# Loads of small tables moved behind a stage's first weight units, x issued from ScalarE's queue

## What is computed

```python
for l in range(2):                                          # first_block
    h = h + 0.5 * swiglu(rms_norm(h, ffn1_norm[l]), ...)    # f1
    h = h + token_mixer(rms_norm(h, mix_norm[l]), ...)      # m
    h = h + 0.5 * swiglu(rms_norm(h, ffn2_norm[l]), ...)    # f2
x = rms_norm(h, final_norm)
for l in range(2):                                          # second_block
    x = x + 0.5 * rmsnorm(swiglu_2(rmsnorm(x, ffn1_pre_g[l]), ...), ffn1_post_g[l])
    ...                                                     # mixer, with mix_post_g
    x = x + 0.5 * rmsnorm(swiglu_2(rmsnorm(x, ffn2_pre_g[l]), ...), ffn2_post_g[l])
```

## Time and profile before

| | |
|---|---|
| median of three runs | 2842.36 us |
| the profiled execution | 2840.82 us, its span 2839.0 us |
| PE busy | 2639.4 us (93%) |
| DVE, ACT busy | 1544.9 us (54%), 1223.6 us (43%) |
| mean granted TensorE clock | 0.958 |
| HBM read | 452.84 MB, 161 GB/s over the span |

### The profile page before, as it was taken

One profiled execution on the slowest core, in us unless ns is written; L12 is line 12 of the kernel. 1 busy time (PEld: TensorE's weight loads), 2 busy tenths in 40 slices (PEclk: granted clock), 3 DMA queues, 4 the chain that ended last, 5 costly groups with the idle time before them and its releaser, 6 DMA issues.

```text
span 2839.0 us, 30036 instructions
## 1 busy us (share of the span) xinstructions
PE 2639.4 (93%) x12238; PEld 2196.0 (77%) x12238; DVE 1544.9 (54%) x1787; ACT 1223.6 (43%) x1530; POOL 48.2 (2%) x71
## 2 busy tenths in 40 slices
PE   7799999989998998898998998899898998998899
PEld 5688778878887887786877877688687877877687
DVE  3445665455565554555556575555454556475544
ACT  3445444444453443444434453444444444453443
POOL 0000000000000000000000000000000000000000
PEclk9899999999999999999998999999999998999999
DMA  7665355555643555655542442554664552432553
GB/s 183 195 226 174 112 167 186 178 169 187 215 163 119 178 190 165 199 185 170 180 169 90 135 134 75 171 192 140 196 192 170 178 164 96 135 134 75 170 183 129
DMA packets 309753, 459.02 MB, mean 162 GB/s; under 512 B 18112, under 2 KB 207856, under 8 KB 309360
## 3 DMA queue, kind: packets, MB, share of 16 engines
q1 hardware_dynamic: 307552, 453.95, 48.8%
q10 hardware_dynamic: 2064, 3.15, 1.0%
HBM read 452.84 MB, written 4.19 MB: 161 GB/s over the span
## 4 chain that ended last, share of the span: by engine, by line
PE 85%; DVE 5%; ACT 3%; DMA 3%; issue 2%; SPq 1%; DVEq 0%; POOL 0%; ACTq 0%
PE acc L586 45%; PE work L586 32%; PE work L593 2%; PE acc L797 2%; ACT w_hi L1024 2%; DMA raw<-ffn_w_dram 1%; PE work L781 1%; DMA raw<-w_ffn_in_dram 1%; DVE w_lo L1331 1%; PE work L993 1%; DVE xt_lo L1355 1%; SPq L366 0%; DVE field L1519 0%; DMA raw<-w_in_dram 0%; PE work L810 0%
## 5 line engine op out<-in xcount | busy, mean ns | idle before, releaser
L1331 DVE TENSOR_TENSOR w_lo<-raw,w_hi 128x2048 fp32r<-128x2048 f32 (+1 forms) x420 | 953.5, 2272 | 879.8 <-ACT w_hi L1024 879.4
L1024 ACT CAST w_hi<-raw 128x2048 fp32r<-128x2048 f32 (+1 forms) x420 | 794.6, 1893 | 693.8 <-PE acc L586 294.6
L586 PE MATMUL work<-w_hi,xt_hi 128*128 128x512 f32 x1408 | 563.7, 400 | 66.8 <-DVE xt_lo L1355 63.8
L586 PE MATMUL work<-w_hi,xt_lo 128*128 128x512 f32 x1408 | 553.8, 393 | 0.0
L586 PE MATMUL work<-w_lo,xt_hi 128*128 128x512 f32 x1408 | 553.4, 393 | 0.0
L586 PE MATMUL acc<-w_hi,yt_hi 128*128 128x512 f32 x1088 | 435.6, 400 | 21.6 <-DVE yt_lo L1342 20.9
L586 PE MATMUL acc<-w_lo,yt_hi 128*128 128x512 f32 x1088 | 430.4, 396 | 0.0
L586 PE MATMUL acc<-w_hi,yt_lo 128*128 128x512 f32 x1088 | 430.0, 395 | 0.0
L586 PE MATMUL acc<-w_hi,xt_hi 128*128 128x512 f32 (+2 forms) x896 | 347.7, 388 | 24.4 <-DVE xt_lo L1355 20.0
L586 PEld LDWEIGHTS work<-w_hi,xt_hi 128*128 128x128 f32 x1408 | 268.0, 190 | 125.5 <-issue 72.6
L586 PE MATMUL acc<-w_hi,xt_lo 128*128 128x512 f32 (+2 forms) x896 | 343.9, 384 | 0.0
(11 more groups left out here) (162 smaller groups left out, 1708.3 us busy)
## 6 DMA issues: line engine op xcount, KB each, us to landing
raw<-ffn_w_dram SPq DMA_DIRECT2D x264, 512.0 KB, 4.5
raw<-w_in_dram SPq DMA_DIRECT2D x204, 512.0 KB, 4.5
raw<-w_ffn_in_dram SPq DMA_DIRECT2D x176, 512.0 KB, 4.8
raw<-w_ffn_out_dram SPq DMA_DIRECT2D x88, 512.0 KB, 4.4
raw<-w_branch_dram SPq DMA_DIRECT2D x48, 512.0 KB, 4.5
raw<-w_out_dram SPq DMA_DIRECT2D x32, 512.0 KB, 4.4
bias<-b_gate_dram SPq DMA_DIRECT2D x10, 512.0 KB, 7.6
raw<-w_branch_attn_dram SPq DMA_DIRECT2D x8, 512.0 KB, 4.0
```

The source lines that it names most:

```text
L586: last = nc.tensor.matmul(out, x[:, kt, k], y, start=start and n == 0, stop=stop and n == 2)
L1024: nc.scalar.copy(w_hi[:, slot, 0:n], raw[:, at, 0:n]).then_inc(hi_split[slot], 1)
L1331: nc.vector.tensor_tensor(w_lo[:, at, 0:n], raw[:, at, 0:n], w_hi[:, slot, 0:n].bitcast(F32), ALU.subtract).then_inc(unit_split[slot], 1)
```

## The change

The small loads of a stage are issued behind its fifth unit (u+4) rather than its second; in `mixer2` behind its fourth. The tables that stood between the blocks are issued with those of the first stage of block 1. The constants and `final_norm` are issued behind the fifth unit of stage 0; x, `ident` and the first gain come from ScalarE's queue, and ACT and DVE turn the first half of row 0 before they split unit 0. The bias table is made at step j = 2 rather than j = 0, in another PSUM bank, and PE no longer waits for its reader.

```diff
             def ffn(block, name, l, between=lambda: None):
                 load(u, gate_up(block, name, l, 0, 0))
                 load(u + 1, gate_up(block, name, l, 0, 4))
-                small(block, l, name)
                 for j in range(steps - 1):
                     load(u + 3 * j + 2, gate_up(block, name, l, j + 1, 0))
                     load(u + 3 * j + 3, gate_up(block, name, l, j + 1, 4))
                     load(u + 3 * j + 4, down(block, name, l, j))
+                    if j == 0:
+                        small(block, l, name)
+                        between()
...
-                chunks("w_in_2", 2576, 1)
+                chunks("w_in_2", 2576, 2)
                 small(1, l, "m")
-                chunks("w_in_2", 3088, 3)
+                chunks("w_in_2", 3600, 2)
...
-            for r in range(2):
-                sp.dma_start(h[:, r, :], a["x"][0, r * P:(r + 1) * P, :]).then_inc(x_loaded[r], 16)
-            sp.dma_start(ident[:, :], a["ident"]).then_inc(ident_loaded, 16)
-            sp.dma_start(vec[:, 0:8], a["gain1"][0]).then_inc(gain1_loaded, 16)
...
+            def constants():
+
+                sp.dma_start(field[0:32, 4096:4112], a["rel_bias_2"]).then_inc(consts_loaded, 16)
...
+                sp.dma_start(post[:, :], a["final_norm"].rearrange("(a n) -> a n", a=1).partition_broadcast(P)) \
+                    .then_inc(post_loaded, 16)
+
+            def second_block():
+
+                sp.wait_ge(h_ready, h_count(number[0, depth - 1, "f2"]))
+                for dst, src in ((decay, a["decay"]), (rope2, a["rope2"])):
+                    sp.dma_start(dst, src).then_inc(blk_loaded, 16)
+                sp.wait_ge(scratch_stored, 16)
...
             for block in range(2):
                 for l in range(depth):
-                    ffn(block, "f1", l)
+                    ffn(block, "f1", l, (second_block if block else constants) if l == 0 else lambda: None)
...
                     if j == 0:
                         turn_hidden(0)
-                        if stage == 0:
-                            pe.wait_ge(consts_loaded, 80)
-                            nc.tensor.matmul(acc[0][0:16, 0:3 * P], field[0:32, 4096:4112], field[0:32, 4200:4584],
+                    if j == 2 and stage == 0:
+                        pe.wait_ge(consts_loaded, 80)
+                        nc.tensor.matmul(work[1][0:16, 0:3 * P], field[0:32, 4096:4112], field[0:32, 4200:4584],
...
-                    if j == 0 and stage == 0:
-                        pe.wait_ge(table_ready, 2)
...
+                elif not stage:
+                    split(0)
                 turn_hi_rows(stage, 0, (2, 3))
+                if not stage:
+                    split(1)
                 split(u + 2)
...
-            split(0)
-            split(1)
+            act.dma_start(h[:, 0, :], a["x"][0, 0:P, :]).then_inc(x_loaded[0], 16)
+            act.dma_start(ident[:, :], a["ident"]).then_inc(ident_loaded, 16)
+            act.dma_start(vec[:, 0:8], a["gain1"][0]).then_inc(gain1_loaded, 16)
+            act.dma_start(h[:, 1, :], a["x"][0, P:2 * P, :]).then_inc(x_loaded[1], 16)
             enter(0)
...
-                    elif stage == 0:
+                    if j == 2 and stage == 0:
                         act.wait_ge(table_ready, 2)
                         act.dma_start(a["scratch"], field[0:16, 5000:5384].unsqueeze(1).broadcast_to([16, P, 3 * P])) \
                             .then_inc(scratch_stored, 16)
```

More of the change, by code:

```diff
@@ L419, in mixer_small, with ffn @@
                         .then_inc(bias_loaded[i], 16)
-            def ffn(block, name, l):
+            def ffn(block, name, l, between=lambda: None):
                 u = first_unit[block, l, name]
@@ L498, in mixer2 @@
                 chunks("w_out_2", 0, 2)
-            for r in range(2):
-                sp.dma_start(h[:, r, :], a["x"][0, r * P:(r + 1) * P, :]).then_inc(x_loaded[r], 16)
-            sp.dma_start(ident[:, :], a["ident"]).then_inc(ident_loaded, 16)
-            sp.dma_start(vec[:, 0:8], a["gain1"][0]).then_inc(gain1_loaded, 16)
-            sp.dma_start(field[0:32, 4096:4112], a["rel_bias_2"]).then_inc(consts_loaded, 16)
-            sp.dma_start(field[0:32, 4200:4584], a["one_hot"]).then_inc(consts_loaded, 16)
@@ L506, in _ @@
-            sp.dma_start(field[0:16, 4600:4984], a["unseen"]).then_inc(consts_loaded, 16)
-            sp.dma_start(causal[:, :], a["causal"]).then_inc(consts_loaded, 16)
-            sp.dma_start(rope1[:, :, :, :], a["rope1"]).then_inc(consts_loaded, 16)
+            def constants():
+                sp.dma_start(field[0:32, 4096:4112], a["rel_bias_2"]).then_inc(consts_loaded, 16)
+                sp.dma_start(field[0:32, 4200:4584], a["one_hot"]).then_inc(consts_loaded, 16)
+                sp.dma_start(field[0:16, 4600:4984], a["unseen"]).then_inc(consts_loaded, 16)
+                sp.dma_start(causal[:, :], a["causal"]).then_inc(consts_loaded, 16)
+                sp.dma_start(rope1[:, :, :, :], a["rope1"]).then_inc(consts_loaded, 16)
+                sp.dma_start(post[:, :], a["final_norm"].rearrange("(a n) -> a n", a=1).partition_broadcast(P)) \
+                    .then_inc(post_loaded, 16)
@@ new lines, in second_block @@
+            def second_block():
[3 more added lines that the diff above has]
+                sp.wait_ge(scratch_stored, 16)
+                sp.dma_start(rel_bias, bass.AP(a["scratch"].tensor, P - 1,
+                                               [[3 * P - 1, P], [3 * P * P, 16], [1, 2 * P]])) \
+                    .then_inc(blk_loaded, 16)
@@ L509, in _ @@
             for block in range(2):
                 for l in range(depth):
-                    ffn(block, "f1", l)
+                    ffn(block, "f1", l, (second_block if block else constants) if l == 0 else lambda: None)
                     (mixer2 if block else mixer1)(l)
                     ffn(block, "f2", l)
[L514 to L523, removed]
-                                                   [[3 * P - 1, P], [3 * P * P, 16], [1, 2 * P]])) \
-                        .then_inc(blk_loaded, 16)
@@ L698, in ffn @@
                         turn_hidden(0)
-                        if stage == 0:
-                            pe.wait_ge(consts_loaded, 80)
-                            nc.tensor.matmul(acc[0][0:16, 0:3 * P], field[0:32, 4096:4112], field[0:32, 4200:4584],
-                                             start=True, stop=True).then_inc(table_ready, 1)
+                    if j == 2 and stage == 0:
+                        pe.wait_ge(consts_loaded, 80)
+                        nc.tensor.matmul(work[1][0:16, 0:3 * P], field[0:32, 4096:4112], field[0:32, 4200:4584],
+                                         start=True, stop=True).then_inc(table_ready, 1)
                     for r in range(2):
                         gate_up_rows(u + 2 + 3 * j, j, 1, r)
-                    if j == 0 and stage == 0:
-                        pe.wait_ge(table_ready, 2)
                     for r in range(2):
@@ L1438, in enter @@
                 else:
-                    turn_lo_rows(stage, 0, range(4))
+                    turn_lo_rows(stage, 0, (0, 1))
+                    split(0)
+                    turn_lo_rows(stage, 0, (2, 3))
+                    split(1)
                 split(u + 2)
@@ L1476, in ffn @@
                         split(u + 5 + 3 * j)
-                    elif stage == 0:
+                    if j == 2 and stage == 0:
                         dve.wait_ge(table_ready, 1)
-                        nc.vector.tensor_tensor(field[0:16, 5000:5384], acc[0][0:16, 0:3 * P], field[0:16, 4600:4984],
+                        nc.vector.tensor_tensor(field[0:16, 5000:5384], work[1][0:16, 0:3 * P], field[0:16, 4600:4984],
                                                 ALU.add).then_inc(table_ready, 1)
```

## The result

The kernel after takes **2754.59 us**, the median of four runs (2753.86 to 2757.64), beside 2841.57 for the kernel before in the same comparison (four runs): a ratio of 0.9698, with an interval of 0.9676 to 0.972. That is 87.0 us less. The forecast was 2754.0. The profiled execution of after took 2757.64 us, span 2755.9, at a mean granted clock of 0.970. The two profiled executions lie 83.1 us apart in their spans.

A forecast was written before the change was run, and what follows sets the result against it. PE was taken to bound the kernel wherever fed, leaving only its idles to win. Boundaries 75.4, switch 6.9, stage 6's tables -0.4, start 6.0 and store 0 sum to 87.9 us less: 2754 us, range 2736 to 2779.

The forecast's parts named there:

- The bound: Whole kernel: PE bounds it wherever fed (85% of the ending chain), so the change wins only where PE stands still.
- Boundaries: Starts of stages 3 and 6 to 11: a unit not yet multiplied holds up `xt_lo`; freeing it gains 75.4 us.
- the forecast's walk: Stage 11, all four engines followed from h at 2638.67: `turn_hidden` at 2654.0 against 2664.38, 10.4 us gained.
- a sign of being wrong: Anywhere: u+5 or the load from scratch becomes the end of PE's waits, or the store's gap moves over 8 us.
- The switch: Between the blocks: PE's 4.2 us wait and 2.7 us of slow products both go, 6.9 us gained.
- The start: Program start: first product at about 12.9 us, 6.0 us earlier, bounds 4.2 to 7.5.
- the rival of 4.2 us by issue time alone: Program start: the second queue saves only issue time, 4.2 us, total 2755.8; chance 0.12.
- The store: Bias table's store in stage 0, costing 20.1 us: moving it from j = 0 to j = 2 gains 0, between -15 and +8.
- The rival of a changed price: Bias table's store: up to 15 us less (2739) or 5.6 us more (2760); chance 0.12.
- The slower rival: Whole kernel: a denser PE is granted less clock, say 0.90 instead of 0.958, giving 2904 us; chance 0.01.
- The boundary rival: Stage starts: boundaries give less, as u+5 lands late or the silu chain is longer; 2778 us, chance 0.18.
- The signs named in advance: Trace: `xt_lo` waits about 1 us, no stage-start cast awaiting DMA, first product near 13 us, 36 us store near 70.

The follow-up runs named there:

- e4: Kernel after with one tiny ScalarE activation ahead of its first real one, to bring the table load forward; 2751.69 us.
- e8: Kernel after with row 0 of x, `ident` and first gain on SyncE's queue ahead of weights, row 1 of x behind unit 1; 2751.37 us.
- e7: Kernel after with store in four parts, block 1's tables spread over stage 6, x on SyncE's queue, and a tiny activation at the start; 2729.25 us.

## Why the prediction was right, and where it was not

**The bound.** Right. PE bound the kernel wherever it was fed, and the edit of the small loads, which touches no product, gave 79.9 us by itself through the seven starts of stages.

**Boundaries.** Right in mechanism and size: 75.0 forecast, 75.7 in the traces. PE resumes 0.77 us late in stage 11 (0.9 forecast), and the clock level of 0.50 behind it is gone, as forecast. In stage 11 the chain from h to `turn_hidden` takes 2581.22 - 2566.87 = 14.35 us, the forecast's walk had 2654.0 - 2638.67 = 15.3, so the silu chain is one us shorter than walked and the boundary gives 11.6, not 10.4. In stage 6 the cover was less than forecast: u+5 lands at 1118.46 + 9.66 = 1128.12, 17.7 us behind h rather than 14.6, and PE waits 2.75 us for it rather than at most 1. The boundary gives 9.85 where 11.9 was counted. What failed in the walk is the start of the tables and not the rate: it counted them as begun when h is complete (1110.4) at 0.35 MB per us, but the windows of after (columns of rows 6) show 153 GB/s in the first five us and 363 in the next, the rate of the earlier trace rows and more.

```profile
1110.00:1115.00 5.00, 4.24 (x22) 3.12 (x22) 4.70 (x10) 5.00 (x13) 3.50 (x4) 1.00 0.54 153
1115.00:1120.00 5.00, 5.00 (x24) 4.14 (x23) 4.36 (x3) 3.15 (x4) 0.00 (x0) 1.00 1.03 363
```

By an estimate from these windows, the 1.0 MB that the first five us moved less than at 0.35 MB per us are 2.8 of the 3.1 us by which u+5 was late. The prediction had named this as a sign of being wrong, "if u+5 or the load from scratch became the end of PE's waits": in stage 6, and only there, u+5 did.

**The switch.** The term of 6.9 us was too large: 3.9. PE now stands for h itself, and behind that the clock is not full: its transposes wait 1.86 us for the final norm's `h`, and the granted clock from 1100 to 1105 us is 0.66 (PE's timeline, the window, columns of rows 6).

```profile
1100.57 1.14 PE L623 MATMUL work<-ident,h 128*128 128x128 f32 x6 [1.86 <-DVE h L1413]
```
```profile
1100.00:1105.00 5.00, 4.42 (x16) 3.51 (x17) 3.16 (x8) 1.14 (x4) 0.00 (x0) 0.66 0.41 139
```

The forecast added the idle and the slow products and did not ask what is late next, though it did so at every boundary. It also put both down to the tables as one; about 2 us of the idle were `final_norm`'s.

**The start.** The term of 6.0 us failed: the pair of traces gives 3.8, just under its lower bound of 4.2, and the means of three and seven executions 40.0 - 35.9 = 4.1. That is near the rival of 4.2 us by issue time alone, but the agreement says nothing for that rival: unit 0, whose first issue moved up by 4.2 us, was cast only 2.1 us earlier in `e4` (8.99, against 11.05), and the order of ACT's and DVE's work changed as well. The walk had `xt_hi` ready before unit 0 was cast. It took all DMAs of the start as one sum of bytes at a common rate, by which the small `ident` would be there early, and it took ACT's table load as hidden, because it was so in before. Both were on the path. Repairing either brought `turn_hidden(0)` to 33.8 and 33.4 us, against 35.9 on the mean.

**The store.** The 0 for its move was right, and so was its price as a whole (20.1 read from the trace, 18 to 20 shown by splitting it). The rival of a changed price falls. Its picture of weights that nearly stop is right for the first part of the store only.

**The slower rival**, a lower granted clock for a denser PE, falls too: the mean rose from 0.958 to 0.970, and to 0.98 in the profiled execution of the densest kernel.

**A slip.** The boundary rival adds "3 us at each of seven, and 5 in stage 6" to 24; six at 3 and one at 5 are 23, seven at 3 and 5 more are 26. It changes nothing here.

**The signs named in advance.** Met: `xt_lo` waits of 0.8 us, `turn_hidden` of stage 11 14.35 us behind h, a store of 35.3 us begun at 71.6 and one wait of 16.2 behind it, L671 without a gap. Not met: the first product at 14.95 rather than near 13, and ACT's cast of u+5 in stage 6.

**The sum.** 87.9 forecast, 87.0 between the medians. The start (-2.2), the switch (-3.0) and the mixers' scatter (-2.2 in the profiled pair) were made up in part by the boundaries (+0.7), the store's stretch (+1.9) and by the distance of the profiled execution from its median. Part of the agreement to 0.6 us is luck; the 75 of the boundaries are not.

## What to carry to other kernels

Where one queue issues in order, look for the wait that stands ahead of prefetch: small tables that must wait for the end of a stage belong behind the weight units whose buffers are already free (here behind the fifth, with five buffers), since a unit that nobody multiplies yet can still hold up activations through the program order of the engines that split it. When an instruction is moved to the front of an engine's program, ask what came for free with the old front: here a table load that was hidden. A long store beside a stream of weights is cheap in parts shorter than the buffers bridge, wherever it stands.

## What the runs showed of the hardware

- ACT's table load goes with the first instruction that needs it, and can end up behind a wait of that instruction: it began at 0.94 us in before, although the cast behind it waited for its unit until 11.05; at 8.35 in after, only when PE's transposes were done; and at 3.00 in front of a small activation put there for it. It took 1.28 us each time. Why it went ahead of the wait in the first case and not in the second, no run shows.
- The store of 3 MB from 16 partitions, each row written 128 times, moves about 88 GB/s. The Trainium skill ("DMA: Bandwidth & Descriptors", Queues, rings and completion order) says that a DMA engine takes turns between the queues it has work for, packet by packet. The trace of after agrees from 92 to 104 us, with 739 packets of either queue; as a packet of the weights is 1.0 KB there and one of the store 1.5, and the weights' take 17.5% of the engines' time and the store's 84.5%, turns are no even share. From 76 to 90 us it shows something else, 895 packets of the store and none of the weights already issued. Why, no run here shows.
- 64 KB of `ident` took 5.0 to 6.3 us when issued from a second queue beside weights (eight executions), and 3.2 and 3.5 us ahead of them on one queue (`e8`, `e7`).
- An idle of PE near 3 us costs clock in some executions and not in others: behind its wait for u+5 in stage 6 PE went on at full clock after 2.75 us in after, and ran at the half level (0.50 from 1133 to 1139 us) after 2.98 us in `e4`.
